# Seven block products in the feed-forward gate and up units of a two-model forward pass in float32

## Chip, cores and metric

One core of one Trainium2 chip. The metric is the device time of one execution in microseconds (us), lower is better. Three runs of the kernel before gave 2111.71, 2114.69 and 2115.12 us, median 2114.69.

## The reference, cut to what matters

The input is one sequence of 512 tokens, 1024 features, float32. Two layers (retention, differential attention) come first; then 16 meta tokens are put in front (528 tokens), and a second model adds half a feed-forward, a mixing layer (latent attention beside a gated delta net) and half of another feed-forward:

```python
def swiglu(x, w_gate, w_up, w_down):
    return (jax.nn.silu(x @ w_gate) * (x @ w_up)) @ w_down      # 1024 -> 2816 -> 1024
# x = x + 0.5 * swiglu(rmsnorm_2(x, ffn_norm), gate, up, down), twice: ffn1 and ffn2
```

ffn1 works on 528 tokens, ffn2 on 512. Only these two are touched by the change.

## The kernel before, in words

Everything on chip is transposed: features on the 128 partitions, tokens along the free dimension. Weights come in **units**, 256 output columns by 8 blocks of 128 input rows (UNIT = 2048 elements a partition, 1 MB). Each float32 product is made of three matmuls on halves of the operands: a high part that the fast float32 format holds exactly, and the rest, low. `hi` (L901, its activation is L899) makes a unit's high part WH on ACT, `lo` (L761, L758) subtracts it on POOL and writes the low part WL over the raw unit. The raw unit is loaded by SP (L626 for gate and up, L608 for down) as soon as PE has finished the unit four before it, since there are four raw buffers (RAWS) and three for the high part (SPLITS).

A feed-forward (`ffn_pe` L2421, `ffn_act` L1123, `ffn_dve` L1648) is cut in parts of 12 and 10 hidden tiles of 128 (FFN_PARTS). In a part, gate and up units alternate, each giving two hidden tiles, then come 8 down units, folded: two units share a pair of output tiles. The order of work on each engine is written out:

- PE (`project`, L2104, every matmul is L2101): per unit, for two column blocks m and eight k, high by high, high by low, low by high; the 528 tokens of ffn1 go as two matmuls of 264. A unit starts when its low part is there (`lo_done`).
- DVE, gate unit (L1662, L1671): product by the inverse norm row RSTDB into SG, and once more after the silu. Up unit (L1665, L1676): SG times product into TMP, then the low part of the hidden tile. Down unit (L1688): half the product is added to the residual.
- ACT (`next_hi`, L906, ahead of each unit's own work): the high part of the weight unit two ahead; then silu (L1138) or the high part of the hidden tile (L1140).
- POOL: `split` (L766), the low part of each unit in order.

PSUM has four slots of two banks of 512 columns; a unit takes two slots, and `ps_free` gives them back. The inputs u_hi and u_lo (UH, UL) are made by ACT and DVE ahead of the feed-forward (L917, L1402). The norm of the input is summed while the first two units run, so that RSTDB is only known late in the second unit.

## Time and profile before

| | us |
|---|---|
| median of 3 runs | 2114.69 |
| lowest, highest run | 2111.71, 2115.12 |
| span of the profiled execution | 2111.5 |
| PE busy / weight loads busy | 2059.4 / 1769.5 |
| DVE / ACT / POOL busy | 817.3 / 736.1 / 761.0 |

The profiled execution's own time is not listed apart; its span of 2111.5 us is 0.2 us under the lowest of the runs. Busy times of PE are modelled (matmuls overlap), so distances between starts are the better measure. In rows of groups the columns are: line, engine, operation, out<-in, shapes, count, busy us and mean ns of one, then the idle time of the engine ahead of them and who ended it. In a timeline they are start, duration, engine, line, operation, count, and in brackets the idle time before and its releaser.

### The profile page before, as it was taken

Reading aid. Unit: us, or ns where it says so; the run is one execution under the profiler, and the core shown is the slowest. Engines: PE = TensorE matmul, PEld = TensorE weight load, DVE = VectorE, ACT = ScalarE, POOL = GpSimd, SP = SyncE. Lnnn points to the kernel's source line nnn. Section 1 sums busy time; section 2 is a strip of 40 time slices with the busy share of each in tenths; the row PEclk is TensorE's granted clock in tenths of the full one; section 3 lists DMA queues with packets and bytes.
Section 4 is the critical chain, followed back from the end, with each engine's and each line's share of the span. In section 5 each row is a group of like instructions: output and inputs, shape, how many; then the busy total and the mean of one; then the engine's idle time right before and its main releaser. Section 6 shows DMA issues by size and latency. Waiting matters only on the chain.

```text
span 2111.5 us, 32172 instructions
## 1 busy us (share of the span) xinstructions
PE 2059.4 (98%) x13992; PEld 1769.5 (84%) x13992; DVE 817.3 (39%) x1300; ACT 736.1 (35%) x1140; POOL 761.0 (36%) x243
## 2 busy tenths in 40 slices
PE   8999999999999999999999999999999999999998
PEld 6899888878977789999999878798777788888886
DVE  4400675145357655220222242266566644211222
ACT  5332222336556544221222344342312323222222
POOL 4433232545310054334333431045243235434432
PEclk9999999999999999999999999999999999999999
DMA  5323122222310122223323431222013223223322
GB/s 173 100 87 109 52 74 80 80 90 81 100 61 21 41 80 81 81 75 106 100 66 94 103 100 31 60 68 81 22 62 111 81 82 98 90 83 107 100 68 72
DMA packets 170052, 171.52 MB, mean 81 GB/s; under 512 B 16940, under 2 KB 160680, under 8 KB 169912
## 3 DMA queue, kind: packets, MB, share of 16 engines
q1 hardware_dynamic: 168508, 167.25, 25.1%
q8 instruction: 110, 1.80, 0.4%
q10 hardware_dynamic: 1404, 2.23, 0.3%
q14 instruction: 30, 0.25, 0.0%
HBM read 163.17 MB, written 6.29 MB: 80 GB/s over the span
## 4 chain that ended last, share of the span: by engine, by line
PE 89%; DVE 4%; issue 3%; ACT 2%; POOL 1%; DMA 1%; ACTq 0%; SPq 0%; DVEq 0%; POOLq 0%
PE ps L2101 87%; PE ps L2103 2%; DMA x_rows<-in_x 0%; ACT diag L927 0%; DVE gdn_x L1966 0%; DVE gdn_inv_t L1949 0%; POOL w_lo L758 0%; POOL stat L775 0%; ACT u_hi L953 0%; DMA ret_decay<-c_decay 0%; ACT w_hi L899 0%; ACT residual L952 0%; DVE gdn_inv_t L1945 0%; DVE tmp L1414 0%; DVE sg L1609 0%
## 5 line engine op out<-in xcount | busy, mean ns | idle before, releaser
L758 POOL TENSOR_TENSOR w_lo<-w_raw,w_hi 128x2048 fp32r<-128x2048 f32 (+3 forms) x153 | 654.8, 4282 | 901.7 <-ACT w_hi L899 896.2
L2101 PE MATMUL ps<-u_hi,w_hi 128*128 128x512 f32 (+1 forms) x1904 | 584.4, 347 | 9.8 <-DVE sg L1609 2.6
L2101 PE MATMUL ps<-u_hi,w_lo 128*128 128x512 f32 (+1 forms) x1904 | 578.6, 344 | 0.0
L2101 PE MATMUL ps<-u_lo,w_hi 128*128 128x512 f32 (+1 forms) x1904 | 569.5, 344 | 1.0 <-DVE u_lo L1402 0.8
L2101 PEld LDWEIGHTS ps<-u_hi,w_hi 128*128 128x128 f32 x1904 | 328.6, 189 | 53.0 <-issue 5.5
L2101 PEld LDWEIGHTS ps<-u_lo,w_hi 128*128 128x128 f32 x1904 | 326.6, 189 | 43.7 <-DVE u_lo L1402 5.5
L2101 PEld LDWEIGHTS ps<-u_hi,w_lo 128*128 128x128 f32 x1904 | 328.1, 189 | 40.0 <-issue 0.5
L899 ACT ACTIVATE w_hi<-w_raw 128x2048 fp32r<-128x2048 f32 (+3 forms) x157 | 279.0, 1779 | 175.0 <-PE ps L2101 168.9
L2101 PE MATMUL ps<-hidden_hi,w_hi 128*128 128x264 f32 (+1 forms) x528 | 141.1, 321 | 0.0
L2101 PE MATMUL ps<-hidden_lo,w_hi 128*128 128x264 f32 (+1 forms) x528 | 141.0, 322 | 0.0
L2101 PE MATMUL ps<-hidden_hi,w_lo 128*128 128x264 f32 (+1 forms) x528 | 140.8, 321 | 0.0
L2101 PE MATMUL ps<-w_lo,u_hi 128*128 128x256 f32 x384 | 107.9, 281 | 0.0
L2101 PE MATMUL ps<-w_hi,u_lo 128*128 128x256 f32 x384 | 107.9, 281 | 0.0
L2101 PE MATMUL ps<-w_hi,u_hi 128*128 128x256 f32 x384 | 107.6, 280 | 0.0
L1688 DVE SCALAR_TENSOR_TENSOR residual<-ps,residual 128x528 f32<-128x528 f32 (+1 forms) x32 | 22.4, 700 | 209.8 <-PE ps L2101 209.8
L1665 DVE TENSOR_TENSOR tmp<-sg,ps 128x528 f32<-128x528 f32 (+1 forms) x44 | 30.5, 696 | 172.9 <-PE ps L2101 172.8
L1662 DVE TENSOR_TENSOR sg<-ps,rstd_row 128x528 f32<-128x528 f32 (+1 forms) x44 | 30.4, 699 | 165.6 <-PE ps L2101 165.6
L2101 PEld LDWEIGHTS ps<-hidden_lo,w_hi 128*128 128x128 f32 x528 | 87.7, 188 | 8.0
L2101 PEld LDWEIGHTS ps<-hidden_hi,w_hi 128*128 128x128 f32 x528 | 87.4, 188 | 7.9
L2101 PEld LDWEIGHTS ps<-hidden_hi,w_lo 128*128 128x128 f32 x528 | 87.6, 188 | 7.7
L1140 ACT ACTIVATE hidden_hi<-tmp 128x528 fp32r<-128x528 f32 (+1 forms) x44 | 28.2, 642 | 176.0 <-DVE tmp L1665 176.0
L1138 ACT ACTIVATE sg<-sg 128x528 f32<-128x528 f32 (+1 forms) x44 | 28.0, 641 | 170.9 <-DVE sg L1662 170.9
(379 smaller groups left out, 2959.8 us busy)
## 6 DMA issues: line engine op xcount, KB each, us to landing
w_raw<-in_w_in_a SPq DMA_DIRECT2D x22, 1024.0 KB, 5.3
w_raw<-in_ffn_w_gate SPq DMA_DIRECT2D x22, 1024.0 KB, 5.4
w_raw<-in_ffn_w_up SPq DMA_DIRECT2D x22, 1024.0 KB, 5.4
w_raw<-in_w_in SPq DMA_DIRECT2D x17, 1024.0 KB, 5.2
...
```

Source lines behind the costliest of these rows:

```text
L758: pool.tensor_tensor(WL[:, u % RAWS, part], RAW[:, u % RAWS, part], WH[:, u % SPLITS, part].bitcast(F32), ALU.subtract).then_inc(lo_done, 1)
L899: nc.scalar.activation(WH[:, u % SPLITS, part], RAW[:, u % RAWS, part], ACT.Copy).then_inc(hi_done, 1)
L1138: nc.scalar.activation(SG[:, m, 0:width], SG[:, m, 0:width], ACT.Silu).then_inc(silu_done, 1)
L1140: nc.scalar.activation(HH[:, 4 * i + 2 * (j // 2) + m, 0:width], TMP[:, m, 0:width], ACT.Copy).then_inc(hh_done, 1)
L1662: nc.vector.tensor_tensor(halves(SG[:, m, 0:width]), acc(slot, width), halves(RSTDB[:, 0:width]), ALU.mult).then_inc(ps_free[slot], 1)
L1665: nc.vector.tensor_tensor(halves(TMP[:, m, 0:width]), halves(SG[:, m, 0:width]), acc(slot, width), ALU.mult).then_inc(ps_free[slot], 1)
L1688: nc.vector.scalar_tensor_tensor(out=halves(RES[:, k, cols]), in0=acc(slot, width), scalar=0.5, in1=halves(RES[:, k, cols]), op0=ALU.mult, ...
L2101: return nc.tensor.matmul(o, a, b, start=start, stop=stop, **kw)
L2103: return nc.tensor.transpose(o, x, IDENT[0:n, 0:n])
```

## The change

FFN_PARTS becomes (6, 6, 6, 4), and a down job is 4 units of the part's 6 or 4 blocks, not folded. Gate and up units, but for the first two of each feed-forward, are computed by a seven-product scheme for 2 x 2 blocks: a unit is four blocks of four k by 128 columns (b11, b12, b21, b22), the input four blocks of four k by half of the tokens. Each product is 4 k x 3 matmuls of 256 or 264 columns. Order in every unit: p1, then p6 and p7 (summed weights by summed inputs), p5, p2, p4, p3. p2, p4 and p3 accumulate on the banks of p1, p7 and p5.

DVE makes three weight sums per unit (four operations, one in place) two units ahead, between the two tiles of the unit at hand; ACT and POOL split them in high and low beside the unit's own halves. Once per feed-forward DVE and ACT make and split three summed inputs, and one block of u_hi and u_lo is overwritten by a fourth sum. The products are joined by DVE (`seven_out`), with a copy of p1 that ACT takes. Four semaphores for table loads are merged to one, which changes no order of work.

```diff
-FFN_PARTS = (12, 10)
+FFN_PARTS = (6, 6, 6, 4)
+ORDER = ("p1", "p6", "p7", "p5", "p2", "p4", "p3")
+FIRST_ORDER = ("p1", "p6", "p7", "p5", "p2", "p4", "p3")
...
+        TF = place("w_sum", [P, 2, 3 * 512], "mix_sum")
+        TL = place("w_sum_lo", [P, 2, 3 * 512], None, F32R, over="w_sum")
+        TH = place("w_sum_hi", [P, 2, 3 * 512], "w_sum", F32R)
+        FIRSTP = place("first_product", [P, HALF], None, over="sq")
...
-            ffns[name] = [(job(part, spread_after=3 if name == "ffn1" and part == FFN_PARTS[0] else None),
-                           job(8, fold=2, kc=part // 2)) for part in FFN_PARTS]
+            ffns[name] = [(job(part, spread_after=3 if name == "ffn1" and n == 0 else None), job(4, kc=part))
+                          for n, part in enumerate(FFN_PARTS)]
...
+        seven_units = [jg.unit0 + n for name in ("ffn1", "ffn2") for part, (jg, _) in enumerate(ffns[name])
+                       for n in range(jg.units) if part or n >= 2]
+        seven_no = {u: v for v, u in enumerate(seven_units)}
+        first_sevens = [ffns[name][0][0].unit0 + 2 for name in ("ffn1", "ffn2")]
...
+                if u in seven_no:
...
+                    pool.wait_ge(sum_hi, 2 * v + 1)
+                    pool.wait_ge(w_summed, 4 * v + 3)
+                    pool.tensor_tensor(WL[:, a, 0:half], RAW[:, a, 0:half], WH[:, b, 0:half].bitcast(F32),
+                                       ALU.subtract).then_inc(sum_lo, 1)
+                    pool.wait_ge(sum_hi, 2 * v + 2)
+                    pool.tensor_tensor(TL[:, e, :], TF[:, e, :], TH[:, e, :].bitcast(F32),
+                                       ALU.subtract).then_inc(sum_lo, 1)
+                    lo_part(u, slice(half, UNIT), u + 2)
+                elif u < n_units:
...
-                hi(jb.unit0 + 4 * i + j + 2)
+                u = jb.unit0 + 4 * i + j
+                if u + 1 in seven_no:
+                    seven_hi(u + 1)
+                if u + 2 not in seven_no:
+                    hi(u + 2)
+            def seven_hi(u):
...
+                act.wait_ge(done, unit_ticks[u - SPLITS])
+                act.wait_ge(w_summed, 4 * v + 2)
+                nc.scalar.activation(WH[:, b, 0:half], RAW[:, a, 0:half], ACT.Copy).then_inc(sum_hi, 1)
+                if v >= 2:
+                    act.wait_ge(done, unit_ticks[seven_units[v - 2]])
+                act.wait_ge(w_summed, 4 * v + 4)
+                nc.scalar.activation(TH[:, e, :], TF[:, e, :], ACT.Copy).then_inc(sum_hi, 1)
+                nc.scalar.activation(WH[:, b, half:UNIT], RAW[:, a, half:UNIT], ACT.Copy).then_inc(hi_done, 1)
...
+                for k in range(k4):
+                    nc.scalar.activation(XF22[:, k, 0:half], RES[:, k4 + k, second_half], ACT.Copy, scale=gain(name, k4 + k))
+                    last = nc.scalar.activation(XF11[:, k, 0:half], RES[:, k, first_half], ACT.Copy, scale=gain(name, k))
+                last.then_inc(mix_hi, 1)
...
+                        if v is not None:
+                            slot, _ = chunk_of(jg, i, j, 0)
+                            act.wait_ge(prod, product_tick(u, "p1"))
+                            if v:
+                                act.wait_ge(joined_done, 4 * (v - 1) + 1)
+                            nc.scalar.activation(FIRSTP[:, 0:half], PS[:, 2 * slot, 0:half], ACT.Copy).then_inc(first_kept, 1)
...
+                        if part == 0 and (i, j) == (0, 0):
+                            for t in range(3):
+                                act.wait_ge(mixed, 8 * number + t + 2)
+                                nc.scalar.activation(SH[:, t, :, 0:half], SF[:, t, :, 0:half], ACT.Copy).then_inc(mix_hi, 1)
+                        if part == 0 and (i, j) == (0, 1):
+                            act.wait_ge(done, unit_ticks[u])
+                            nc.scalar.activation(UH[:, 0:k4, second_half], XS1[:, :, 0:half], ACT.Copy).then_inc(mix_hi, 1)
...
+            def w_sums(u):
...
+                b11, b12, b21, b22 = [raw[:, KC // 2 * i:KC // 2 * (i + 1), P * j:P * (j + 1)] for i in range(2) for j in range(2)]
+                t2, t3, t4 = [TF[:, e, 512 * n:512 * (n + 1)].rearrange("p (c n) -> p c n", c=KC // 2) for n in range(3)]
...
+                if v >= 2:
+                    dve.wait_ge(done, unit_ticks[seven_units[v - 2]])
+                nc.vector.tensor_tensor(t3, b12, b22, ALU.subtract).then_inc(w_summed, 1)
+                dve.wait_ge(w_summed, 4 * v + 1)
+                nc.vector.tensor_tensor(b12, b12, b11, ALU.subtract).then_inc(w_summed, 1)
+                dve.wait_ge(w_summed, 4 * v + 2)
+                nc.vector.tensor_tensor(t2, b12, b22, ALU.subtract).then_inc(w_summed, 1)
+                dve.wait_ge(w_summed, 4 * v + 3)
+                nc.vector.tensor_tensor(t4, b21, t2, ALU.add).then_inc(w_summed, 1)
+            def mix_sums(name, number):
...
+                dve.wait_ge(mix_hi, 5 * number + 1)
+                for n, (out, at_k, part, other, op) in enumerate((
+                        (XS1, 0, second_half, XF22, ALU.add), (SF[:, 0], 0, first_half, XS1, ALU.subtract),
+                        (SF[:, 1], 0, second_half, XF11, ALU.subtract), (SF[:, 2], k4, first_half, SF[:, 0], ALU.add))):
+                    if n in (1, 3):
+                        dve.wait_ge(mixed, 8 * number + n)
...
+                        last = nc.vector.scalar_tensor_tensor(out=out[:, k, 0:half], in0=RES[:, at_k + k, part],
+                                                              scalar=gain(name, at_k + k), in1=other[:, k, 0:half],
+                                                              op0=ALU.mult, op1=op)
+                    last.then_inc(mixed, 1)
...
+                    def seven_out(i, j):
...
+                        x, y, z, w = [PS[:, b, 0:half] for b in (2 * s0, 2 * s0 + 1, 2 * s1, 2 * s1 + 1)]
...
+                        dst = SG if gate else TMP
+                        def factor(m, part_cols):
+                            return RSTDB[:, part_cols] if gate else SG[:, m, part_cols]
+                        dve.wait_ge(first_kept, v + 1)
+                        dve.wait_ge(prod, product_tick(u, "p6"))
+                        nc.vector.tensor_tensor(U2[:, low], FIRSTP[:, low], y, ALU.add).then_inc(joined_done, 1)
+                        dve.wait_ge(prod, product_tick(u, "p7"))
+                        dve.wait_ge(joined_done, 4 * v + 1)
+                        nc.vector.tensor_tensor(U3[:, low], U2[:, low], w, ALU.add).then_inc(joined_done, 1)
+                        dve.wait_ge(prod, product_tick(u, "p5"))
+                        dve.wait_ge(joined_done, 4 * v + 2)
+                        nc.vector.tensor_tensor(dst[:, 1, high], U3[:, low], z, ALU.add).then_inc(joined_done, 1)
...
+                        dve.wait_ge(prod, product_tick(u, "p2"))
+                        nc.vector.tensor_tensor(dst[:, 0, low], factor(0, low), x, ALU.mult).then_inc(ps_free[s0], 1)
+                        dve.wait_ge(prod, product_tick(u, "p4"))
+                        nc.vector.tensor_tensor(dst[:, 0, high], U2[:, low], w, ALU.add).then_inc(joined_done, 1)
+                        dve.wait_ge(joined_done, 4 * v + 4)
+                        nc.vector.tensor_tensor(dst[:, 0, high], dst[:, 0, high], factor(0, high),
+                                                ALU.mult).then_inc(chunk_ready, 1)
+                        dve.wait_ge(done, unit_ticks[u])
+                        dve.wait_ge(joined_done, 4 * v + 3)
+                        nc.vector.tensor_tensor(dst[:, 1, low], U2[:, low], z, ALU.add).then_inc(ps_free[s1], 1)
+                        dve.wait_ge(ps_free[s1], uses1 + 1)
+                        nc.vector.tensor_tensor(dst[:, 1, 0:width], dst[:, 1, 0:width], factor(1, slice(0, width)),
+                                                ALU.mult).then_inc(chunk_ready, 1)
...
+                            if j == 0:
+                                mix_sums(name, number)
...
+                            if m == 0:
+                                w_sums(u + 2)
...
+                                dve.wait_ge(mix_hi, 5 * number + t + 2)
+                                nc.vector.tensor_tensor(SL[:, t, :, 0:half], SF[:, t, :, 0:half],
+                                                        SH[:, t, :, 0:half].bitcast(F32), ALU.subtract).then_inc(mixed, 1)
+                        if part == 0 and (i, j) == (0, 1):
...
+                            dve.wait_ge(mix_hi, 5 * number + 5)
+                            nc.vector.tensor_tensor(UL[:, 0:k4, c], XS1[:, :, 0:half], UH[:, 0:k4, c].bitcast(F32),
+                                                    ALU.subtract).then_inc(mixed, 1)
...
+                        w_sums(jd.unit0 + j + 2)
...
+                made = {"p1": (own(0, 0), plain(0, low), x, True), "p5": (own(0, 1), plain(0, high), z, True),
+                        "p6": (summed(0), mixed_in(0), y, True), "p7": (summed(1), mixed_in(1), w, True),
+                        "p2": (own(1, 0), plain(k4, low), x, False), "p4": (summed(2), plain(k4, high), w, False),
+                        "p3": (own(1, 1), mixed_in(2), z, False)}
+                new_input = u in first_sevens
...
+                    if name == "p1":
+                        pe.wait_ge(sum_lo, 2 * v + 1)
+                        slot_free(pe, s0, uses0)
+                        slot_free(pe, s1, uses1)
+                    if name == "p6":
+                        pe.wait_ge(sum_lo, 2 * v + 2)
+                        if new_input:
+                            pe.wait_ge(mixed, 8 * number + 5)
+                    if name == "p7" and new_input:
+                        pe.wait_ge(mixed, 8 * number + 7)
+                    if name == "p5" and new_input:
+                        pe.wait_ge(mixed, 8 * number + 8)
+                    if name == "p2":
+                        pe.wait_ge(lo_done, u + 2)
+                        pe.wait_ge(first_kept, v + 1)
+                    if name == "p4":
+                        pe.wait_ge(joined_done, 4 * v + 2)
+                    if name == "p3":
+                        pe.wait_ge(joined_done, 4 * v + 3)
+                    weights, moving, bank, first = made[name]
...
+                        mm(o, wh, xh, start=first and k == 0, stop=False, skip_group_check=not first)
+                        mm(o, wh, xl, start=False, stop=False, skip_group_check=not first)
+                        last = mm(o, wl, xh, start=False, stop=k == k4 - 1, skip_group_check=not first)
...
+                        last.then_inc(done, 2)
+                    else:
+                        last.then_inc(prod, 1)
...
-                    project(jg, UH, UL, cols, k_ready=(ul_done, applied[name]), after=None if part else name)
-                    project(jd, HH, HL, hcols, kc=FFN_PARTS[part] // 2,
-                            k_ready=(hl_done, 22 * number + (FFN_PARTS[0] if part else 0)))
+                    if part == 0:
+                        project(jg, UH, UL, cols, k_ready=(ul_done, applied[name]), after=name, units=range(2))
+                    for n in range(jg.units):
+                        if jg.unit0 + n in seven_no:
+                            seven(name, number, jg, n, cols)
+                    project(jd, HH, HL, hcols, kc=FFN_PARTS[part], k_ready=(hl_done, tiles_before(number, part)))
```

## Rows read from the trace of the kernel before

**Rows 1.** The page: span, and busy time of each engine.
```profile
span 2111.5 us, 32172 instructions
PE 2059.4 (98%) x13992; PEld 1769.5 (84%) x13992; DVE 817.3 (39%) x1300; ACT 736.1 (35%) x1140; POOL 761.0 (36%) x243
```

**Rows 2.** The page, the chain that ended last: shares by engine.
```profile
PE 89%; DVE 4%; issue 3%; ACT 2%; POOL 1%; DMA 1%; ACTq 0%; SPq 0%; DVEq 0%; POOLq 0%
```

**Rows 3.** Windows: length, busy us (instructions) of PE, PEld, DVE, ACT, POOL; clock, DMA.
```profile
538.00:550.00 12.00, 12.00 (x104) 12.00 (x103) 4.97 (x2) 6.04 (x8) 4.63 (x1) 1.00 0.28 87
```

**Rows 4.** Timeline of SP: weight load issues (start, us, engine, line, operation).
```profile
827.47 0.37 SPq L626 DMA_DIRECT2D w_raw<-in_ffn_w_gate  x1
839.21 0.37 SPq L626 DMA_DIRECT2D w_raw<-in_ffn_w_up  x1
...
1752.96 0.37 SPq L626 DMA_DIRECT2D w_raw<-in_ffn_w_up  x1
1786.32 0.37 SPq L626 DMA_DIRECT2D w_raw<-in_ffn_w_gate  x1
1797.44 0.37 SPq L626 DMA_DIRECT2D w_raw<-in_ffn_w_up  x1
```

**Rows 5.** Groups by shape, POOL: weight splits.
```profile
L758 POOL TENSOR_TENSOR w_lo<-w_raw,w_hi 128x2048 fp32r<-128x2048 f32 x117 | 541.8, 4634 | 699.5 <-ACT w_hi L899 694.0 <-DVE gdn_out_lo L2056 5.5
L758 POOL TENSOR_TENSOR w_lo<-w_raw,w_hi 128x1536 fp32r<-128x1536 f32 x16 | 56.1, 3509 | 92.7 <-ACT w_hi L899 92.7
L758 POOL TENSOR_TENSOR w_lo<-w_raw,w_hi 128x1024 fp32r<-128x1024 f32 x4 | 9.6, 2401 | 23.7 <-ACT w_hi L899 23.7
```

**Rows 6.** Groups by shape, DVE: one operand in PSUM, 512 and 256 elements.
```profile
L1966 DVE TENSOR_TENSOR gdn_x<-ps,gdn_tri 128x256 f32<-128x256 f32 x40 | 16.7, 423 | 5.6 <-PE ps L2101 4.7
L1665 DVE TENSOR_TENSOR tmp<-sg,ps 128x512 f32<-128x512 f32 x22 | 15.1, 688 | 84.2 <-PE ps L2101 84.2
```

**Rows 7.** Groups by shape, ACT: split, silu, copy out of PSUM.
```profile
L899 ACT ACTIVATE w_hi<-w_raw 128x2048 fp32r<-128x2048 f32 x121 | 230.9, 1910 | 81.1 <-PE ps L2101 75.0 <-DVE ret_scores L1490 5.6
L1138 ACT ACTIVATE sg<-sg 128x512 f32<-128x512 f32 x22 | 13.9, 635 | 85.4 <-DVE sg L1662 85.4
L987 ACT ACTIVATE ret_v<-ps,stat 128x256 f32<-128x256 f32 x32 | 13.5, 472 | 62.4 <-PE ps L2101 62.4
```

**Rows 8.** Timeline of DVE, start of ffn2.
```profile
1748.14 1.29 DVE L1662 TENSOR_TENSOR sg<-ps,rstd_row 128x512 f32<-128x512 f32 x2
...
1753.58 8.63 DVE L1676 TENSOR_TENSOR hidden_lo<-tmp,hidden_hi 128x512 fp32r<-128x512 f32 x2
...
1764.70 1.48 DVE L1671 TENSOR_TENSOR sg<-sg,rstd_row 128x512 f32<-128x512 f32 x2
...
1780.77 0.69 DVE L1662 TENSOR_TENSOR sg<-ps,rstd_row 128x512 f32<-128x512 f32 x1 [3.48 <-PE ps L2101]
```

**Rows 9.** Timeline of POOL, the same stretch.
```profile
1751.98 9.68 POOL L758 TENSOR_TENSOR w_lo<-w_raw,w_hi 128x2048 fp32r<-128x2048 f32 x2 [2.03 <-ACT w_hi L899]
...
1778.45 4.62 POOL L758 TENSOR_TENSOR w_lo<-w_raw,w_hi 128x2048 fp32r<-128x2048 f32 x1 [6.50 <-ACT w_hi L899]
```

**Rows 10.** By tile, 1751 to 1764: durations min/median/max of the colliding operations.
```profile
L1676 DVE TENSOR_TENSOR hidden_lo<-tmp,hidden_hi x2: 3591/4352/5114, 1753.6 to 1757.1; 128x512 fp32r<-128x512 f32 x2
...
L758 POOL TENSOR_TENSOR w_lo<-w_raw,w_hi x2: 4637/4864/5090, 1752.0 to 1756.6; 128x2048 fp32r<-128x2048 f32 x2
```

**Rows 11.** Timeline of DVE, start of ffn1.
```profile
810.54 8.28 DVE L1671 TENSOR_TENSOR sg<-sg,rstd_row 128x528 f32<-128x528 f32 x2 [0.42 <-ACT sg L1138]
```

**Rows 12.** Windows, and timeline of PE, around the gap at 1236.
```profile
1237.30:1240.70 3.40, 3.40 (x11) 2.58 (x10) 1.60 (x3) 2.19 (x2) 0.00 (x0) 0.53 0.48 165
...
1236.42 1.13 PE L2101 MATMUL ps<-diag,ones 88*128 88x264 f32 x4 [2.12 <-ACT diag L927]
1237.71 0.63 PE L2101 MATMUL ps<-cq_lo,w_hi 128*128 128x512 f32 x1
1238.14 0.63 PE L2101 MATMUL ps<-cq_hi,w_lo 128*128 128x512 f32 x1
```

182 lines of the change are left out of this document (136 added, 46 removed).

## Prediction

> **What bounds the kernel now.** I read the page's totals first: TensorE (PE) is busy 98% of a span of 2111.5 us, DVE 39%, POOL 36% [rows 1]. Then the chain that ended last: 89% of it lies on PE [rows 2]. So a gate or up unit costs what its matmuls cost, and other engines cost nothing while they keep ahead. A unit of ffn2 (48 matmuls of 512 columns) takes 11.12 us from one weight load issue to the next, one of ffn1 (96 of 264) 11.74 us [rows 4]: 0.232 and 0.1223 us a matmul. 256 columns take 0.1165 us in the stretch with 103 weight loads in 12 us [rows 3]; I take 0.117. The clock was at its upper level (1.00, 2.4 GHz) there [rows 3].
>
> The second thing to see is what DVE and POOL do to each other. A DVE operation that reads one operand from PSUM takes 0.69 us at 512 elements [rows 6], also when POOL is in the middle of a weight split (DVE at 1780.77 inside POOL's 1778.45 to 1783.07) [rows 8, 9]. A DVE operation with both inputs in SBUF does not. At 1753.58 two such, of 0.74 us each when alone (1.48 for two), took 8.63 us for the pair while POOL ran two splits from 1751.98 to 1761.66 [rows 8, 9]; singly 3.59 and 5.11 us, and each ended about 0.6 us after a POOL split [rows 10]. ffn1 has the same: 8.28 us for two [rows 11]. POOL's second split was longer by 5.09 - 4.64 = 0.45 us [rows 10]. So the two take turns, whole instructions at a time.
>
> **The change, part by part.** *PE.* 20 of 22 units of each feed-forward take 84 half-width matmuls: ffn1 84 x 0.1223 = 10.28 us, ffn2 84 x 0.117 = 9.85. With no new wait that is 20 x 1.46 + 20 x 1.27 = 55 us less. The down matmuls keep their number (528 at 512 columns a feed-forward, or twice that at 264). One product is 1.40 us in ffn2, 1.47 in ffn1.
>
> *POOL.* One split of 2048 (4.63 us) becomes 1024 + 1536 + 1024: 2.40 + 3.51 + 2.40 = 8.31 us [rows 5].
>
> *ACT.* Split 0.96 + 1.48 + 0.96, copy of the first product 0.47, two passes 1.28 [rows 7]: 5.2 us of 10, and it stays hidden; the cover is PE's unit.
>
> *DVE.* Added per unit: four weight sums of 512, chained by their own semaphore (4 x 0.74 = 2.95 us), seven half-width operations of 0.42 (the 256-wide row, [rows 6]) and one full-width (0.69) in place of two of 0.69; the two later operations of 0.69 stay. In all 8.0 us: under 9.85, if nothing blocks. But of these the weight sums, the half-width and the full-width multiplication by the factor and the two later ones have both inputs in SBUF, and POOL now needs 8.31 us of the same unit.
>
> **Turns in one unit.** POOL 8.31; the chained weight sums 2.95 (POOL can't start the next unit's first split before the third sum); the scaling ahead of them 0.65; and three that come between POOL's splits, at what such a turn added to POOL, 0.45 + 0.45 + 0.30. Together 13.1 us, against PE's 9.85. The price of a turn lies between 0.45 [rows 10] and a whole operation of 0.69, so 13.1 to 13.8; nothing excludes that POOL slips in cheaper where DVE waits for PE, which would leave some 12.5. I take 13.1, as the only direct row of a turn.
>
> The Trainium skill (SBUF — State Buffer, § Who interferes with whom) says that the loser of this port is blocked for the whole instruction; by it each of the three turns costs its full length, the unit is 13.7 us, and the total some 10 us more. The 0.45 us of the trace disagree with the full 0.69, and the trace decides.
>
> *Where PE stands still.* With X the end of a unit's weight sums: POOL's first split to 2.4, DVE's last operation of the unit before to 2.95, U2 and U3 to 3.8. Product p4 needs U3, so p4 and p3 run 3.85 to 6.65; POOL's 3.5 us ends near 6.3, its last split near 8.9; DVE's wide multiplication is blocked to 9.45, scaling 10.1, sums 13.1: the next X. PE ends p3 at X + 6.65 and the next unit's first five products (7.0) at X + 13.65, but U3 comes at the next X + 3.8, that is X + 16.9: a gap of 3.2 us a unit.
>
> *A run of 6* (parts two and three) by this, in ffn2, from PE's last down matmul: the first unit (A) was split under the down units: 9.85. B's X is at 18.85 (its sums wait behind POOL's splits for A, the three turns of A follow): end 25.5. C, D, E + 13.1 each: 64.8. F has no weight sums ahead of it: 74.65. Before: 6 x 11.12 = 66.7. So +7.9. A run of 4: 48.45 against 44.5, +4.0. In ffn1 the same with 10.28 and 11.74: +5.1 and +2.2.
>
> *The first part of each feed-forward.* T is PE's end with the second plain unit (weight load issued at 1752.96, [rows 4]). DVE's input sums, 16 of half width at 0.42, start at T - 3.6, behind its first two products, and end T + 3.8 with a POOL split in the way; scaling and weight sums for A to 7.4. Then turns: POOL 2.4, DVE 0.6, POOL 3.5, DVE 1.1 (1024 wide, estimated from the 512 and 256 rows: 0.69 + 2 x 0.27 = 1.2 alone, a turn 0.1 less), POOL 2.4, DVE 2.2: 19.6. The up unit's own 2.4, sums for B 2.9: 24.9. POOL 2.4, DVE 0.6, POOL 3.5, then u_lo of the sum 1.1: 32.4. p5 of A waits for exactly this; four products later A ends at T + 38 where 9.85 was possible. DVE then needs 5 us more to the next X (43.0); B ends 49.65, C 62.75, D 72.6, against 44.5: +28. ffn1: +26.5. All of this hangs on the new input operands being queued on DVE between gate, up and weight work.
>
> *Clock.* One PE gap in the middle of the kernel is as long: 2.12 us at 1236.42. Behind it the granted clock was 0.53 (the lower level, 1.2 GHz) in 3.4 us, and 512-column matmuls came every 0.43 us instead of 0.232 [rows 12]. That costs 1.5 us per gap, but inside a run it falls into the time in which DVE is blocked anyway; it shows once per run and twice in first parts: +15 us. Between 0 and 1.5 us in each of 26 gaps: 0 to 39.
>
> *Down units, ends of parts.* The last hidden tiles are needed 2.8 and 3.5 us into the down job instead of much later; U2 to split takes about 2.7 us behind PE: nothing, at most 2 us in 8 parts each. The cover is the first four k of the job. Residual additions double (16 more of 0.69 a feed-forward), hidden in down units of 8.3 us.
>
> **Sum.** ffn2 28 + 2 x 7.9 + 4.0 = 48; ffn1 26.5 + 2 x 5.1 + 2.2 = 39; clock 15: +102 on the profiled span of 2111.5, 2213. The execution around that span is the lowest of the three runs shown (2111.7) or close to it, 3 us under their median. I predict 2214 us.
>
> **Rivals.**
> 1. *PE stays the bound (faster).* If DVE and POOL fit between each other, the unit stays at 9.85 and 10.28. Place: the turns in one unit; it decides when their sum is under 9.85 us. Gain 55; the first parts still wait, as DVE has work of its own up to T + 18.7 (input and weight sums 8.1, splits of the sums 3.7, up tile 2.0, sums for B and its last split 3.7, u_lo 1.2) ahead of p5, which PE wants at 4.2: 2 x 14.5 = 29 back. 2111.5 - 26 = 2085. For it: DVE's sum of 8.0 and idle rows before; against: every row of a collision. 0.11.
> 2. *The clock stays low.* With a 3 us gap in every unit, matmuls could run at the lower level between gaps too: a product 1.4 x 0.43 / 0.232 = 2.6 us, a unit 18.2. All 40: 2111.5 + 728 - 457 (what they take now) = 2382; half of them, 2300. For it: the only such gap; against: the clock came back after 3.4 us of work. 0.08.
> 3. *Cheaper turns.* POOL's splits mostly fall where DVE waits for PE; the middle units take 11.5 (28 x 0.1 more than now), first and last ones of a run gain 1.3 to 1.5 (12, -17), the first parts' entries cost 2 x 28: 2111.5 + 3 - 17 + 56 = 2153. 0.15.
> 4. *Only the weight sums hurt and entries are short* (the input operands ready early): within 0.2%, near 2113. 0.02.
> My forecast has 0.64.
>
> **Range and chances.** The forecast's own range is 2180 to 2250 (turn 0.69 and clock in every gap above; no clock and 12.5 us below). Reaching to rival 3: 2138 to 2255. 0.2% is about what a measurement of this kernel can tell from no change. Faster 0.11, same 0.02, slower 0.87.
>
> **What would show it.** Right: TensorE below 95% busy; PE gaps of about 3 us before the ps matmuls of p4, released by DVE's U3; gate and up weight loads some 13 us apart; DVE's weight sums, wide multiplications and hidden_lo at means well over 0.69; POOL busy some 140 us more; two waits of 10 us and more released by the u_lo of the sum; clock under 0.97. Wrong: unit distances of 10 us, or two-SBUF operations at 0.7 us beside POOL.

## The result, and the profile after

The changed kernel takes 2218.27 us, the median of 4 runs (2217.59 to 2219.15); the kernel before takes 2114.76 beside it. The ratio is 1.0494, 95% interval 1.0479 to 1.0509: 4.9% slower. The profiled execution has a span of 2216.7 us against 2111.5 [rows 1], 105.2 us more. That is the difference to be explained.

From the page of the kernel after: the totals, and the chain that ended last by engine.

```profile
span 2216.7 us, 34183 instructions
PE 2054.1 (93%) x14472; PEld 1797.5 (81%) x14472; DVE 1222.3 (55%) x1772; ACT 827.4 (37%) x1284; POOL 931.3 (42%) x323
PE 75%; DVE 16%; issue 6%; ACT 2%; POOL 1%; DMA 1%; ACTq 0%; SPq 0%; DVEq 0%; POOLq 0%
```

PE's share of the chain falls from 89% [rows 2] to 75%, and DVE stands in it with 16%. The list of PE's waits (who released it: us in total, times, longest) names what PE was waiting for:

```profile
PE ps L2286 <- DVE three_products L1804: 70.8, 29, 4.2
PE ps L2286 <- DVE tmp L1836: 15.4, 1, 15.4
PE ps L2286 <- DVE u_lo L1863: 10.0, 2, 9.0
PE ps L2286 <- POOL w_lo L807: 8.7, 1, 8.7
PE ps L2286 <- DVE mix_lo L1858: 3.6, 2, 2.1
```

The first line is the wait ahead of p4, for U3: 29 times, 2.4 us in the mean. The other four lines are waits in the two first parts. The distances between SP's weight loads (each is issued when PE ends a unit) show the pattern of a run of 6 units in ffn2's second part. Queue rows, start and length of the issue:

```profile
1916.30 0.37 SPq L659 DMA_DIRECT2D w_raw<-in_ffn_w_gate  x1
1933.40 0.37 SPq L659 DMA_DIRECT2D w_raw<-in_ffn_w_up  x1
1944.80 0.37 SPq L664 DMA_DIRECT2D w_raw<-in_ffn_w_down  x1
1958.93 0.37 SPq L664 DMA_DIRECT2D w_raw<-in_ffn_w_down  x1
1970.62 0.37 SPq L664 DMA_DIRECT2D w_raw<-in_ffn_w_down  x1
1986.36 0.37 SPq L664 DMA_DIRECT2D w_raw<-in_ffn_w_down  x1
```

Unit A ends at 1916.30 after 9.94 us, as PE alone would have it; then B 17.10, C 11.40, D 14.13, E 11.69, F 15.74, where every unit took 11.12 before [rows 4]. Together 80.0 us against 66.7. Why, is seen in one unit of DVE and POOL (timeline; the bracket is idle time ahead and what ended it):

```profile
1963.06 0.69 DVE L1759 TENSOR_TENSOR w_sum<-w_raw,w_sum 128x512 f32<-128x512 f32 x1
1963.56 2.46 POOL L807 TENSOR_TENSOR w_lo<-w_raw,w_hi 128x1024 fp32r<-128x1024 f32 x1 [4.52 <-ACT w_hi L972]
1963.67 2.90 DVE L1849 TENSOR_TENSOR hidden_lo<-tmp,hidden_hi 128x512 fp32r<-128x512 f32 x1
1965.99 3.93 POOL L810 TENSOR_TENSOR w_sum_lo<-w_sum,w_sum_hi 128x1536 fp32r<-128x1536 f32 x1
1966.50 0.41 DVE L1801 TENSOR_TENSOR two_products<-first_product,ps 128x256 f32<-128x256 f32 x1
1967.01 0.42 DVE L1804 TENSOR_TENSOR three_products<-two_products,ps 128x256 f32<-128x256 f32 x1
1969.66 0.54 DVE L1815 TENSOR_TENSOR sg<-sg,rstd_row 128x256 f32<-128x256 f32 x1
1969.88 10.35 POOL L796 TENSOR_TENSOR w_lo<-w_raw,w_hi 128x1024 fp32r<-128x1024 f32 x3
1971.08 1.93 DVE L1821 TENSOR_TENSOR sg<-sg,rstd_row 128x512 f32<-128x512 f32 x1
1972.93 7.85 DVE L1844 TENSOR_TENSOR sg<-sg,rstd_row 128x512 f32<-128x512 f32 x2
1980.71 0.41 DVE L1801 TENSOR_TENSOR two_products<-first_product,ps 128x256 f32<-128x256 f32 x1
```

hidden_lo has both inputs in SBUF: it starts 0.11 us behind POOL's split, lasts 2.90 us instead of 0.69 and ends half a microsecond behind the end of that split. The two additions after it read PSUM and take 0.41 and 0.42 us in the middle of POOL's next split. The lower rows are the end of the run: POOL has its last split and those of two down units ready, runs the three back to back, and DVE's two scalings together take 7.85 us. U2 of the last unit stands behind them. By kind and shape (busy us, mean ns):

```profile
L1844 DVE TENSOR_TENSOR sg<-sg,rstd_row 128x512 f32<-128x512 f32 x22 | 47.5, 2172 | 0.1
L1849 DVE TENSOR_TENSOR hidden_lo<-tmp,hidden_hi 128x512 fp32r<-128x512 f32 x22 | 30.5, 1387 | 0.5
L807 POOL TENSOR_TENSOR w_lo<-w_raw,w_hi 128x1024 fp32r<-128x1024 f32 x40 | 98.1, 2453 | 255.4 <-ACT w_hi L972 255.4
L810 POOL TENSOR_TENSOR w_sum_lo<-w_sum,w_sum_hi 128x1536 fp32r<-128x1536 f32 x40 | 152.5, 3812 | 0.0
```

These means mix two cases. A subtraction or scaling of DVE in this kernel takes either 0.7 us or, where it meets a split, 2.8 us and more: the 44 scalings of L1844 have 20 of 0.68 to 0.71 us, 18 of 2.84 to 2.92 and 6 of 3.9 to 4.0. POOL's split of 1536 takes 3.49 to 3.51 us in 12 units, as before (3.51, [rows 5]), 3.86 to 3.96 in 27 and 4.51 in one: a turn of DVE in front of it costs POOL some 0.4 us. On its first split POOL pays 0.05 us (2.40 before).

### The profile page after: what moved, and what is told of

The parts are those of the page before. It is cut to its first block, busy times and chain, and to the rows that moved or that the text cites. A ratio compares the mean times of both kernels' runs of the same rounds, so it can differ in the third digit from the quotient of the medians.

```text
span 2216.7 us, 34183 instructions
## 1 busy us (share of the span) xinstructions
PE 2054.1 (93%) x14472; PEld 1797.5 (81%) x14472; DVE 1222.3 (55%) x1772; ACT 827.4 (37%) x1284; POOL 931.3 (42%) x323
## 4 chain that ended last, share of the span: by engine, by line
PE 75%; DVE 16%; issue 6%; ACT 2%; POOL 1%; DMA 1%; ACTq 0%; SPq 0%; DVEq 0%; POOLq 0%
PE ps L2286 73%; DVE sg L1844 3%; DVE hidden_lo L1849 2%; PE ps L2288 2%; DVE mix_lo L1858 1%; DVE w_sum L1757 1%; DVE w_raw L1755 1%; DVE w_sum L1753 1%; DVE mix_sum L1773 1%; DVE three_products L1804 1%; DVE sg L1821 1%; DVE two_products L1801 0%; DMA x_rows<-in_x 0%; DVE u_lo L1863 0%; ACT diag L996 0%
## 5 line engine op out<-in xcount | busy, mean ns | idle before, releaser
L796 POOL TENSOR_TENSOR w_lo<-w_raw,w_hi 128x2048 fp32r<-128x2048 f32 (+2 forms) x153 | 577.7, 3782 | 588.7 <-ACT w_hi L949 583.2
L2286 PE MATMUL ps<-u_hi,w_hi 128*128 128x512 f32 (+2 forms) x1424 | 468.0, 345 | 43.9 <-DVE tmp L1836 15.4
L2286 PE MATMUL ps<-u_hi,w_lo 128*128 128x512 f32 (+2 forms) x1424 | 461.2, 341 | 0.0
L2286 PE MATMUL ps<-u_lo,w_hi 128*128 128x512 f32 (+2 forms) x1424 | 453.6, 341 | 1.0 <-DVE u_lo L1495 0.8
L2286 PEld LDWEIGHTS ps<-u_hi,w_hi 128*128 128x128 f32 x1424 | 263.2, 192 | 73.9 <-issue 21.1
L2286 PEld LDWEIGHTS ps<-u_hi,w_lo 128*128 128x128 f32 x1424 | 262.9, 192 | 26.4 <-issue 0.5
L949 ACT ACTIVATE w_hi<-w_raw 128x2048 fp32r<-128x2048 f32 (+2 forms) x117 | 202.5, 1733 | 68.3 <-PE ps L2286 62.4
L807 POOL TENSOR_TENSOR w_lo<-w_raw,w_hi 128x1024 fp32r<-128x1024 f32 x40 | 98.1, 2453 | 255.4 <-ACT w_hi L972 255.4
L810 POOL TENSOR_TENSOR w_sum_lo<-w_sum,w_sum_hi 128x1536 fp32r<-128x1536 f32 x40 | 152.5, 3812 | 0.0
L972 ACT ACTIVATE w_hi<-w_raw 128x1024 fp32r<-128x1024 f32 x40 | 42.4, 1061 | 149.2 <-DVE w_raw L1755 149.2
L2286 PE MATMUL ps<-mix_hi,w_sum_hi 128*128 128x264 f32 (+1 forms) x320 | 92.7, 290 | 4.0 <-DVE mix_lo L1858 3.6
```

Of the source, the lines that this page charges most:

```text
L796: pool.tensor_tensor(WL[:, u % RAWS, part], RAW[:, u % RAWS, part], WH[:, u % SPLITS, part].bitcast(F32), ALU.subtract).then_inc(lo_done, 1)
L807: pool.tensor_tensor(WL[:, a, 0:half], RAW[:, a, 0:half], WH[:, b, 0:half].bitcast(F32), ALU.subtract).then_inc(sum_lo, 1)
L810: pool.tensor_tensor(TL[:, e, :], TF[:, e, :], TH[:, e, :].bitcast(F32), ALU.subtract).then_inc(sum_lo, 1)
L949: nc.scalar.activation(WH[:, u % SPLITS, part], RAW[:, u % RAWS, part], ACT.Copy).then_inc(hi_done, 1)
L972: nc.scalar.activation(WH[:, b, 0:half], RAW[:, a, 0:half], ACT.Copy).then_inc(sum_hi, 1)
L2286: return nc.tensor.matmul(o, a, b, start=start, stop=stop, **kw)
```

## Experiments

**Three causes against each other.** Theory 1: POOL's splits and those operations of DVE that have both inputs in SBUF take turns, and the sum of the turns is the period. ("The port" below is the name for what they take turns at.) Theory 2: DVE's own work or chain is the period. Theory 3: the clock lost in the gaps is a large share by itself.

POOL's work cut to a quarter, DVE's and PE's as they are. Three copies on ACT, which fill the rest, are not in this excerpt:

```diff
-pool.tensor_tensor(WL[:, a, 0:half], RAW[:, a, 0:half], WH[:, b, 0:half].bitcast(F32),
+pool.tensor_tensor(WL[:, a, 0:half // 4], RAW[:, a, 0:half // 4], WH[:, b, 0:half // 4].bitcast(F32),
                    ALU.subtract).then_inc(sum_lo, 1)
...
-pool.tensor_tensor(TL[:, e, :], TF[:, e, :], TH[:, e, :].bitcast(F32),
+pool.tensor_tensor(TL[:, e, 0:384], TF[:, e, 0:384], TH[:, e, 0:384].bitcast(F32),
                    ALU.subtract).then_inc(sum_lo, 1)
-lo_part(u, slice(half, UNIT), u + 2)
+lo_part(u, slice(half, half + half // 4), u + 2)
```

> In the seven-product units POOL's three splits are cut to a quarter of their columns (1024 + 1536 + 1024 elements become 256 + 384 + 256); the rest of the low parts is filled by copies on ScalarE (ACT), so the low parts hold unsplit weights and the output is not the reference's. The work of PE and of VectorE (DVE) is what it was; ACT gets some 2.5 us more a unit. Theory 1 (POOL's splits and DVE's operations with both inputs in SBUF take turns, and their sum of 13.1 us is the period): the sum falls to about 7 us, under PE's 9.85 or 10.28, so the middle units run at PE's pace and U2, U3, the scaling and the weight sums fall to 0.3 to 0.8 us each; the time falls from 2218 to between 2085 and 2110, the first parts keeping part of their wait. Theory 2 (DVE's own chain of dependent operations sets the period, whoever uses the memory): no more than 15 us less, 2203 or above. Theory 3 (the clock lost in the gaps is a large share by itself) goes with 1: it says only that the granted clock rises to over 0.99.

Measured 2111.48 us (10 runs, 2106.91 to 2117.76), ratio to the kernel before 0.9986 (0.9974 to 0.9998): 107 us under the changed kernel. Four middle units in one window (columns: us, busy of PE, PEld, DVE, ACT, POOL, granted clock, DMA share, GB/s), and then the last unit of the same run:

```profile
1852.26:1892.00 39.74, 39.74 (x338) 39.74 (x338) 29.74 (x56) 31.16 (x37) 9.54 (x12) 1.00 0.31 94
1892.00:1906.31 14.31, 11.40 (x85) 11.20 (x84) 10.92 (x10) 4.36 (x6) 7.87 (x3) 0.90 0.17 57
```

9.94 us a unit, PE without a gap, with DVE's work unchanged: theory 2 falls. DVE is busy 7.5 us in each of these units and 10.6 in units C to E of the changed kernel, with the same operations: 3.1 us of blocked time a unit are gone. The last unit still takes 14.3, because the splits of the down units (not cut) stand in it as before; the first parts too keep 13 and 14 us of wait. That is why the time ends at 2111, just above the expected range of 2085 to 2110. The clock of this execution was 0.985, not over 0.99.

More DVE work that has one operand in PSUM:

```diff
+for n in range(3):
...
+    nc.vector.tensor_tensor(dst[:, 1, high], U3[:, low], y, ALU.add).then_inc(reads, 1)
 dve.wait_ge(prod, product_tick(u, "p5"))
```

> In every seven-product unit DVE gets three more half-width additions (0.4 us each, 1.3 us in all) with one operand in PSUM, between U3 and the next addition; their result is overwritten, the output stays. 40 units x 1.3 us = 52 us of DVE work. Theory 1 (turns with POOL): they fall into time in which DVE would wait for PE or for POOL's split, and use the memory port that is not shared; product p3 comes 0.3 us later at most: 2218 to 2230. Theory 2 (DVE's amount or chain is the bound): 40 to 52 us more, 2258 to 2270.

Measured 2201.64 us (2200.06 to 2202.76), ratio 1.0405 (1.0390 to 1.0421): 52 us of work more and 17 us *less* time. Theory 2 is out; that it would become faster, neither theory had said, and theory 1's own range of 2218 to 2230 is missed too. The middle units are a little slower: 12.1, 14.4 and 12.0 us in ffn2's second part, and 3 us more over the twelve units C to E of the four runs of 6. The last units of the parts are faster: the six of the first three parts of each feed-forward take 66.7 us together, where they took 79.2 (15.74 became 11.28, 16.70 became 11.30; two of 10 became 11.3), and the two of the fourth parts 20.4 for 25.7. That is 17.9 us less, as much as the whole difference. The additions delay DVE's multiplication of 256 elements until after POOL's split has begun, and from then on each of the two gets a turn:

```profile
1960.95 6.03 POOL L797 TENSOR_TENSOR w_lo<-w_raw,w_hi 128x1024 fp32r<-128x1024 f32 x2
1961.02 2.61 DVE L1820 TENSOR_TENSOR sg<-sg,rstd_row 128x256 f32<-128x256 f32 x1
1963.99 3.54 DVE L1826 TENSOR_TENSOR sg<-sg,rstd_row 128x512 f32<-128x512 f32 x1
```

Both multiplications are over by 1967.53, and only the scalings behind them are left, instead of falling under the train of three. No run isolates this order, but it divides the last units of four kernels without an exception. In the changed kernel itself the last unit of ffn2's third part took 9.93 us, and there the same multiplication (L1815) starts behind POOL's split, which begins at 2082.71:

```profile
2083.38 1.97 DVE L1815 TENSOR_TENSOR sg<-sg,rstd_row 128x256 f32<-128x256 f32 x1
2085.72 3.54 DVE L1821 TENSOR_TENSOR sg<-sg,rstd_row 128x512 f32<-128x512 f32 x1
2089.19 1.47 DVE L1844 TENSOR_TENSOR sg<-sg,rstd_row 128x512 f32<-128x512 f32 x2
```

In the slow one shown above it starts at 1969.66, 0.22 us ahead of the split at 1969.88. The changed kernel, this one and two of those below (p5 twice, sevens from unit 4) have 32 last units together. In 19 the multiplication starts 0.13 to 0.23 us ahead of the split, and the unit takes 12.1 to 16.7 us; in 13 it starts 0.06 to 1.2 us behind it, and the unit takes 9.9 to 11.3.

More PE work in the gap:

```diff
-for k in range(k4):
+twice = name == "p5" and n not in (0, jb.units - 1) and not new_input
+for k in list(range(k4)) * (2 if twice else 1):
```

> In 24 middle seven units (not the first two, not the last of a run) product p5 is computed twice over (12 more matmuls of 256 or 264 columns, 1.40 or 1.47 us of PE; the output stays). Theory 1: PE stands still there for 1.4 to 3 us a unit anyway, so the 34 us of work cost at most 10: 2218 to 2228. If PE were the bound: 2252. Theory 3 (the clock lost behind the gaps is worth 15 us or more by itself): the gaps shrink, the granted clock rises and the time falls under 2210.

Measured 2224.50 us (2221.01 to 2228.73), ratio 1.0519 (1.0503 to 1.0535): 34 us of matmuls cost 6. This is a net figure: in this kernel all six last units of the first three parts are slow ones, 97.7 us for 79.2, and the rest became 12 us shorter. Units C to E of ffn2's second part, in the changed kernel and then in this one:

```profile
1933.40:1970.62 37.22, 32.48 (x254) 31.87 (x254) 31.41 (x42) 16.47 (x20) 24.62 (x9) 0.95 0.22 72
```

```profile
1938.93:1976.08 37.15, 34.83 (x290) 34.22 (x289) 31.99 (x43) 16.86 (x20) 25.15 (x10) 1.00 0.24 72
```

The same 37.2 us with 254 matmuls at a clock of 0.95 and with 290 at 1.00. In the other three runs of 6 the three units take 37.1, 37.2 and 37.3 us where they took 38.6, 37.1 and 38.2. PE's work does not set this period, and theory 3 has at most 1.5 us a run in the middle units.

Splits moved from POOL (2.40 us each) to DVE (1.22 us each):

```diff
-pool.tensor_tensor(WL[:, a, 0:half], RAW[:, a, 0:half], WH[:, b, 0:half].bitcast(F32),
-                   ALU.subtract).then_inc(sum_lo, 1)
...
-lo_part(u, slice(half, UNIT), u + 2)
...
+nc.vector.tensor_tensor(WL[:, a, c], RAW[:, a, c], WH[:, b, c].bitcast(F32), ALU.subtract).then_inc(own_lo, 1)
...
 nc.vector.tensor_tensor(dst[:, 1, high], U3[:, low], z, ALU.add).then_inc(joined_done, 1)
+own_split(u + 1, 0)
...
                         ALU.mult).then_inc(chunk_ready, 1)
+own_split(u + 1, 1)
```

> In every seven unit the two splits of 1024 move from POOL (2.40 us each) to DVE (estimated at 1.25 us each: the 512 row of 0.69 and 0.27 for each further 256); POOL keeps the one of 1536 (3.5 us). The output stays. Theory 1: the period is the sum of what uses both inputs from SBUF on the two engines: 3.5 + 2.95 + 2.5 + 0.65 + 0.69 + 0.42 + 0.69 = 11.4 us against 12.6 measured: 1.2 us less in 32 units, and 2 to 5 less in the last ones: about 2170. Theory 2 (DVE's amount sets the period): 2.5 us more in each of 40 units, 2318.

Measured 2175.75 us (2175.16 to 2176.85), ratio 1.0295 (1.0281 to 1.0309): 42 us less than the changed kernel, though DVE has 2.5 us more work a unit. Theory 2's 2318 is far off. But the working was wrong in its parts: a middle unit takes 12.92 us, not 11.4.

```profile
1922.24:1935.16 12.92, 10.47 (x84) 10.06 (x84) 12.54 (x17) 6.41 (x7) 3.58 (x3) 1.00 0.20 63
```

And the timeline at its end:

```profile
1932.17 3.50 POOL L808 TENSOR_TENSOR w_sum_lo<-w_sum,w_sum_hi 128x1536 fp32r<-128x1536 f32 x1 [5.94 <-ACT w_sum_hi L975]
1932.41 4.35 DVE L1771 TENSOR_TENSOR w_lo<-w_raw,w_hi 128x1024 fp32r<-128x1024 f32 x1
```

DVE is occupied for 12.54 of 12.92 us: its split of 1.22 us stands blocked for the 3.1 us that are left of POOL's, and operations with an operand in PSUM stand queued behind it. PE's list of waits is led by DVE's own split, 51.4 us in 24 waits. The sum of the turns was 11.4, but DVE's queue held its other work back meanwhile. So the sum of the turns alone does not give the period. The gain came from the second units (11.4 in ffn1 for 16.1 to 16.6, 11.8 to 12.2 in ffn2 for 17.1) and the first parts (A 25.6 for 29.6, 28.6 for 37.3). The total near 2170 is so a right sum of wrong parts.

**The first parts.** The first four units plain, sevens from unit 4:

```diff
-for n in range(jg.units) if part or n >= 2]
+for n in range(jg.units) if part or n >= 4]
```

> The first part of each feed-forward takes its first four units plain and starts the seven products with unit 4; the input sums are still made at unit 0, and the sum that goes into the u operand is written at unit 3, ahead of that unit's hidden tiles. Everything else stays, the output too. Theory 1: two plain units more (2 x 11.12 or 2 x 11.74), then a first seven unit that finds its inputs ready (about 9.9 or 10.2) and one that waits as the second unit of the later parts does (17.1 or 16.0): first part 49.3 us in ffn2 against 77.8, 49.7 in ffn1 against 65.6, so 44 us less: 2174. Rival (the input sums and the first part's wait cost the same wherever they stand, since DVE has that work to do before any seven unit): no more than 10 us less, 2208 or above.

Measured 2190.47 us (2189.26 to 2190.59), ratio 1.0352 (1.0336 to 1.0367): 28 us less, neither 44 nor 10; neither side of the expectation holds. In ffn2 the first part took 54.5 us from T to the end (1786.77 to 1841.30) against 77.8: plain units of 11.69 and 18.01, sevens of 14.89 and 9.94. The two sevens cost less than the 27.0 expected, but the second plain unit costs 18.0 instead of 11.1. The sums hold up plain units too.

**How many sevens the port can carry.** Only the gate units by seven products:

```diff
-for n in range(jg.units) if part or n >= 2]
+for n in range(jg.units) if n % 2 == 0 and (part or n >= 2)]
```

> Only the gate units are taken by seven products; the up units are plain again, with one split of 2048. 20 of the 40 seven units are left. The plain up units read the u operand in which the second half of the first four tiles has been replaced by a sum, so the output is not the reference's. Theory 1: over a pair of units POOL has 8.3 + 4.6 us and DVE 2.95 + 0.65 + turns + 1.4, some 19 us, under PE's 20.97 (ffn2) or 22.02 (ffn1): the pair runs at PE's pace, runs of 6 take 62.9 and 66.1 and of 4 41.9 and 44.0, so the later parts are 22 us under the kernel before; the first parts still wait for the sums, 25 and 16 us over it: about 2135. If a seven unit cost its loss by itself (105 us over 40 units): half of it stays, 2164 or above.

Measured 2152.15 us (2148.47 to 2152.97), ratio 1.0173 (1.0156 to 1.0190), 17 us above the 2135 of theory 1 and 12 below the 2164 of the rival: neither. The first parts cost 20 us in ffn1 and 23 in ffn2 over plain ones, close to what was expected. In the later parts the pair nearly keeps PE's pace, but the seven unit takes 11.58, not 9.94. Its window:

```profile
1888.22:1899.80 11.58, 10.20 (x85) 9.98 (x84) 9.87 (x9) 1.53 (x3) 6.98 (x2) 1.00 0.28 92
```

The timeline of the next such unit, up to p4's first matmul:

```profile
1910.48 11.34 POOL L796 TENSOR_TENSOR w_lo<-w_raw,w_hi 128x1024 fp32r<-128x1024 f32 x3
1911.55 6.91 DVE L1849 TENSOR_TENSOR hidden_lo<-tmp,hidden_hi 128x512 fp32r<-128x512 f32 x2
1918.38 0.41 DVE L1801 TENSOR_TENSOR two_products<-first_product,ps 128x256 f32<-128x256 f32 x1
1919.37 0.39 PE L2286 MATMUL ps<-u_hi,w_sum_hi 128*128 128x256 f32 x1 [1.38 <-DVE three_products L1804]
```

The up unit's hidden_lo pair takes 6.91 us for 1.4 of work, U2 is queued behind it, and p4 comes 1.38 us late. Nobody needs hidden_lo at that time. Two kernels that leave nothing out test this, first with a wholly plain first part and the fourth sum in a place of its own, then with hidden_lo moved too:

```diff
+U4H = place("mix_fourth_hi", [P, KC // 2, HALF], "w_sum_hi", F32R)
...
-for n in range(jg.units) if n % 2 == 0 and (part or n >= 2)]
+for n in range(jg.units) if n % 2 == 0 and part]
```

> The whole first part of each feed-forward is plain, and in the later parts only the gate units use seven products (16 of them). The input sums are made beside the plain units of the first part, and the fourth sum has a place of its own instead of the u operand's, so every output is right. Theory 1 (the loss lies in the first part's entry and in the turns): the later parts go as in the kernel with seven gates and plain ups (66.5 and 43.8 us in ffn2, 67.8 and 44.8 in ffn1) and the first parts as before: 9 us under the kernel before, 2106. Against it: if part of the loss came with the four parts or with the down units, the time would stay over 2120.

```diff
 nc.vector.tensor_tensor(dst[:, 1, high], U3[:, low], z, ALU.add).then_inc(joined_done, 1)
+if late:
+    for args in late:
+        hidden_low(*args)
```

> As the kernel with seven gates in the later parts, and with one thing moved in DVE's queue: the two hidden_lo subtractions of an up unit (both inputs in SBUF) stand behind the additions U2, U3 and their follower of the next gate unit instead of ahead of them. Theory 1: the 1.4 us before p4 come from these two, which wait 7 us for POOL's three splits in a row; moved back, the gate unit takes PE's own 9.95 or 10.2, a run of 6 63.3 or 65.9, of 4 42.2 or 43.9: 21 us under the kernel before, 2093. If the 1.4 us have another source (an unrelated wait of PE): no difference from the kernel without the move, 2106.

Measured 2125.68 us (2122.40 to 2127.28; ratio 1.0056, 1.0044 to 1.0069) and 2111.17 (2109.34 to 2112.44, 11 runs; ratio 0.9985, 0.9976 to 0.9993). The move is worth 14.5 us, and gives the unit back to PE:

```profile
1857.32:1867.26 9.94, 9.94 (x85) 9.93 (x85) 4.68 (x9) 1.52 (x3) 6.52 (x2) 1.00 0.33 105
```

Both totals were 18 to 20 us above what was expected, while the later parts took just the expected times. The rest was again the first part: in the second kernel 57.9 us in ffn1 where four plain units take 47.0, and 17.7 for one of 11.1 in ffn2. PE's list of waits names the up tile of unit 1 in ffn1:

```profile
PE ps L2302 <- DVE tmp L1850: 7.9, 1, 7.9
```

After it the granted clock was 0.81 in the mean of the 15 us from 830.00 to 845.00, with PE busy throughout.

In ffn2 the profile names no releaser ("issue"), but the timeline shows the three splits of the input sums on DVE, blocked by POOL, and PE going on 0.7 us behind their end at 1766.91, which is where DVE's tmp stands next:

```profile
1759.07 7.84 DVE L1872 TENSOR_TENSOR mix_lo<-mix_sum,mix_hi 128x1024 fp32r<-128x1024 f32 x3
1767.60 0.77 PE L2302 MATMUL ps<-u_hi,w_hi 128*128 128x512 f32 x1 [4.80 <-issue]
```

So the input sums were spread (the diff is against the kernel just before):

```diff
-if part == 0 and (i, j) == (0, 0):
-    mix_sums(name, number)
+if part == 0 and i == 0 and j < 2:
+    mix_sums(name, number, (2 * j, 2 * j + 1))
+if part == 0 and (i, j) == (0, 3):
+    split_sum(1)
+    split_sum(2)
+if part == 0 and (i, j) == (0, 2):
+    split_sum(0)
```

> As the kernel with seven gates in the later parts and the late hidden_lo, with the input sums spread over the plain first part: two of the four sums behind unit 0, two behind unit 1, their splits behind units 2 and 3, where all stood behind units 0 and 1. Every output is right. In that kernel PE waited for the up tile of unit 1 (DVE's tmp), 10.9 us with the clock in ffn1 (57.9 us for four units and down to the first down issue, against 47.0) and 6.6 in ffn2 (17.7 against 11.1). If this queueing on DVE is the whole cause, both go: 2111 - 17 = 2094, 0.9% under the kernel before. If the sums cost the same wherever they stand (POOL's splits in between delay the whole row): 2105 to 2112.

Measured 2098.41 us (2097.81 to 2099.64), ratio 0.9929 (0.9915 to 0.9942): 0.7% faster than the kernel before and 5.4% faster than the changed one, with 16 of the 40 seven-product units. It is 4 us above the 2094 expected: the wait in ffn2 is gone, the one for the up tile in ffn1 is still 3.2 us, in place of 7.9:

```profile
PE ps L2307 <- DVE tmp L1852: 3.2, 1, 3.2
```

**The price of a turn by itself.** In the kernel before, three DVE additions more per gate unit, of four sizes:

```diff
+for r in range(3):
+    dve.wait_ge(more, at + r)
+    nc.vector.tensor_tensor(PAD[:, 0:cells, 0:w], UH[:, 0:cells, 16:16 + w].bitcast(F32),
+                            UL[:, 0:cells, 16:16 + w].bitcast(F32), ALU.add).then_inc(more, 1)
```

> The kernel before, with three more DVE additions in every gate unit, both inputs in SBUF, chained, result unused, of 128 elements in ffn1's first part, 256 in its second, 512 and 1024 in ffn2's. They stand in the middle of POOL's split (ACT's silu and the splits run there), and PE stays the bound: 2112 to 2120. Theory 1: each waits for the end of a POOL instruction; POOL's next split is longer by about one DVE instruction less some 0.25 us: next to nothing at 128 (0.2 us each), 0.45 at 512, 1.0 at 1024. If the two engines shared the memory port evenly instead (interleaved), a DVE addition would last up to twice its length alone and never several us.

One run, 2117.63 us. For the most part a miss: the additions did not stand in the middle of POOL's splits but mostly ahead of them. None of the 18 of 128 elements met one, and one of the 15 of 256 did (3.06 us for 0.42). Of the 15 of 1024 elements five took 3.9 to 5.7 us for 1.22, and of the 18 of 512 six took 3.9 to 5.0 us for 0.69 (by tile, min/median/max in ns):

```profile
L1685 DVE TENSOR_TENSOR pad<-u_hi,u_lo x18: 678/692/5005, 1755.4 to 1860.9; 128x512 f32<-128x512 f32 x18
```

One collision in the timeline:

```profile
1771.29 6.45 DVE L1685 TENSOR_TENSOR pad<-u_hi,u_lo 128x512 f32<-128x512 f32 x3
1771.72 4.74 POOL L760 TENSOR_TENSOR w_lo<-w_raw,w_hi 128x2048 fp32r<-128x2048 f32 x1 [1.51 <-ACT w_hi L901]
```

Three additions, some 2.1 us alone, took 6.45, while POOL's split took 4.74 us for 4.62. Under an even sharing no single addition would last more than twice its length; 5.0 us for 0.69 excludes it. What a turn costs POOL by the size of DVE's operation stays open.

## Why the prediction was right, point by point

It said 2214 us and the time is 2218. The mechanism holds: cutting POOL's share takes the loss away, and more DVE work with an operand in PSUM or more PE work in the gap adds next to nothing to the middle units. That the total comes so close is luck in part, since the parts miss by more than that in both directions. The terms:

- *One unit, 13.1 us.* Between the ends of two rows of weight sums lie 13.18 us in one unit (1950.57 to 1963.75), but the units C to E of the four runs of 6 take 12.4, 12.7, 12.9 and 12.4 us in the mean. The mis-sized term is the turns on POOL's side: 1.2 us were put in (0.45 + 0.45 + 0.30, from [rows 10]); POOL's three splits have means of 2.45, 3.81 and 2.60 us, 0.55 over 8.31, since one turn a unit costs it some 0.4 us and the other two little. With that, 8.31 + 0.55 + 2.95 + 0.65 = 12.5, and the lower bound of the text, "some 12.5", was the better value. But this sum has a wrong part too. In all 40 units POOL's first split is released by ACT's split of the unit's first half (L972), which follows DVE's second weight sum, and not by DVE's later sums; the text had ACT hidden. The rows from one middle unit to the next:

```profile
2075.28 1.06 ACT L972 ACTIVATE w_hi<-w_raw 128x1024 fp32r<-128x1024 f32 x1 [1.11 <-DVE w_raw L1755]
2076.42 2.45 POOL L807 TENSOR_TENSOR w_lo<-w_raw,w_hi 128x1024 fp32r<-128x1024 f32 x1 [3.73 <-ACT w_hi L972]
```

  The 3.73 us in which POOL is idle are the end of the DVE multiplication that its last split had blocked (0.55), one hidden_lo (0.6), two weight sums (1.4), ACT's split (1.06) and a short pause. 8.9 + 3.73 is the 12.6 us between two starts of POOL's first split (2063.81 and 2076.42). So the period is a loop through POOL, DVE and ACT, and turns are a part of it.
- *Gap of 3.2 us before p4, released by U3.* 29 gaps, 2.4 us in the mean, 4.2 the longest.
- *B, 15.65 us and 1.5 of clock.* 17.10, 17.11 and 17.14 in ffn2, 16.05 to 16.6 in ffn1.
- *F, 9.85 us, "no weight sums ahead of it".* **This step failed.** In the sum it is 9.85 (10.28 in ffn1). F took 15.74 and 9.93 in ffn2's runs of 6, 10.22 and 16.70 in ffn1's; the last unit of ffn2's first part took 16.45. All eight last units together took 24 us more than the sum had. F has no weight sums, but POOL's splits of two down units stand in their place, and DVE's scalings wait behind them, in the five of eight where DVE's multiplication starts ahead of the split. The twelve units C to E took 151.1 us for the 157.2 of the sum. C, D and E shorter and F longer than in the sum made up for each other in part: 80.0 and 75.1 us in ffn2 against the 76.1 predicted with its clock.
- *First parts, +28 and +26.5 us, 1.5 to 3 of clock on top.* +33.3 and +18.6. In ffn2 the chain ran as told: p5 waits for u_lo until T + 29.96 (32.4 predicted), A ends at T + 37.3 (38); D, the last unit, added its 16.45. In ffn1 DVE had finished the input sums at T - 0.4 and not at T + 3.8, and A ended at T + 29.6: PE stood there once for 15.4 us behind the up tile, a wait that the prediction did not have, and only 1.05 for u_lo.

The waits of A in ffn2, and the window of A with its clock:

```profile
1803.79 0.58 PE L2286 MATMUL ps<-u_hi,w_hi 128*128 128x256 f32 x1 [8.71 <-POOL w_lo L807]
1825.07 0.58 PE L2286 MATMUL ps<-u_hi,w_hi 128*128 128x256 f32 x1 [8.95 <-DVE u_lo L1863]
```

```profile
1795.11:1832.44 37.33, 16.14 (x86) 15.28 (x87) 31.96 (x32) 12.87 (x14) 19.14 (x6) 0.59 0.09 28
```

- *Clock, +15 us.* The mean granted clock is 0.967 (0.995 before). PE was busy 2054.1 us with 14472 matmuls; with the same number and POOL's work cut, 2021.9. That kernel's clock was 0.985. So some 32 us of matmul time go with the lower clock, but part of it lies in gaps that would be idle anyway. Its share of the end time was not isolated.
- *Runs in sum.* The parts measured over the kernel before: ffn2 +33.3, +13.3, +8.4, +7.6; ffn1 +18.6, +4.6, +9.5, +3.5: 98.8 us, against 87 and 15 of clock. 6.4 us lie outside these.
- *Rivals.* "PE stays the bound" needed a sum of turns under 9.85 us; the kernel with a quarter of POOL's work is just that case in its middle units (9.94 us), and its 2111 is 26 us above that rival's 2085, with first and last units still late. "The clock stays low" did not come: C to E had 0.95 to 1.00. "Cheaper turns" had 11.5 us for a middle unit and 2153 in all: turns were cheaper, but the unit took 12.4 to 12.9.
- *Signs.* TensorE at 93%, gaps before p4 released by U3, wide multiplications (2.1 us in the gate units of ffn2) and hidden_lo (1.4) well over 0.69, and a clock of 0.967 came as told. The weight sums did not: of the first two, 37 of 40 took 0.68 to 0.81 us, and the other two took 0.69. POOL was busy 170 us more and not 140. Of the two waits for u_lo one was 8.95 us and the other 1.05, where two of 10 and more were named.

The Trainium skill (SBUF — State Buffer, § Who interferes with whom) says that a DVE instruction with two SBUF inputs contends with a GpSimd instruction that reads SBUF, and one with at most one SBUF input, outside its two-port modes, does not. The runs agree on both: 2.90 us for 0.69 beside a split, and 120 added additions with an operand in PSUM that all took 0.42 or 0.43 us. Of the loser it says that it is blocked for the whole instruction; that is what DVE's rows show as loser, while a turn of DVE's 0.69 us made POOL's split only some 0.4 us longer, and the trace decides for the sum.
